# Reordering the recurrent pairs of a two-layer hybrid diffusion trunk: where the next pair's ScalarE work, one corner product and the ada sums are placed

## Chip, cores and metric

The kernel runs on one NeuronCore of one Trainium2 chip, in float32 throughout. The metric is the device time of one execution in microseconds (us), here the median of the runs shown. Engines are named as in the profile: PE (TensorE matmul), PEld (its weight loads), DVE (VectorE), ACT (ScalarE), POOL (GpSimd), SP (SyncE, which issues the weight DMAs). The granted clock of TensorE is at its upper level (2.4 GHz) in nearly the whole run, 0.994 on average.

## What is computed

Two trunk layers over 256 context tokens and 256 latent tokens of width 1024. Each layer modulates and normalises its input, projects it, runs three branches (a short convolution, a two-directional RWKV-7 recurrence, windowed attention), merges them, and ends in a convolved feed-forward. Layer 1 emits the latent tokens only.

```python
mod_l = jnp.split((jax.nn.silu(c) @ p['ada_w'] + p['ada_b'])[:, None, :], 6, axis=-1)
mod_c = jnp.split(jax.nn.silu(c_ctx) @ p['ada_w'] + p['ada_b'], 6, axis=-1)
hl = modulate(xl, p['norm1_g'], mod_l[0], mod_l[1])
...
def step(S, inp):                       # 16 heads, two directions
    rt, wt, kt, vt, at, bt = inp
    sa = jnp.einsum('dbhvk,dbhk->dbhv', S, at)
    S = S * wt[..., None, :] + sa[..., :, None] * bt[..., None, :] + vt[..., :, None] * kt[..., None, :]
...
w_log = -jax.nn.softplus(-w_pre.astype(f)) - 0.5
decay = jnp.exp(-jnp.exp(w_log))
a = jax.nn.sigmoid((p['rwkv_a0'] + jnp.einsum('tdr,drc->tdc', al, p['rwkv_a2'])).astype(f))
...
xl = xl + mod_l[2] * merge_branches(conv_l, rwkv_l, att_l, gate_l, p)
xl = xl + mod_l[5] * conv_ffn(modulate(xl, p['norm2_g'], mod_l[3], mod_l[4]), p)
```

## The kernel before, in words

Activations lie transposed, 128 channels on the partitions and 512 tokens (T) on the free axis, of which layer 1 mostly uses the last 256 (`lo`). Weights come from HBM as strips of 1024x128 through a ring of five buffers; eight matmuls of one strip (`strip_steps`, L453) make one 128-channel output. **The order of every engine's work is written out by hand**, in one block per engine, and the engines meet by semaphores. PSUM is handed out in three rotations of two slots each: A (emptied by ACT), G (dense projections) and P, called Q in the code (pair work, emptied mostly by DVE). `take(F, name)` waits until the slot's last content has been emptied.

*The recurrence* (`mix`) goes over eight pairs of heads. The tokens are cut into eight chunks of 64. For a pair `i` TensorE does, in this order: products of the chunks (`pair_products`, L676), transposes (`turn_hats` L653, `turn_values` L666), `half_step` (slot `w`, L694: 64 products of 32x32 blocks), `corners` (slot `tl`, L704: 64 products; then slot `tr`, L709: 32 products, the second corner product), `below_left` (slot `x10`, L721), `value_products` (slots `mv0`, `mv1`, L744), `corner_below` (slot `t10`, L730), `bonus_sums` (L750), and for the next pair `key_sums` (L621) and `decays` (L628 twice, then `g`, L631), then `through_inverse` (slots `lrb0` to `lrb3`, L762). After that it walks the chunks: `state_out` (L793) and `state_in` (L779) in turn, seven and seven. Between all these stand the next pair's dense strips, cut into pieces: `fill(steps, n)` issues n units, a unit being one matmul of 256 columns, and `hop` is the number of units between two state steps.

ACT empties the A slots (`corners` L1465 for tl, L1467 and L1468 for tr; `value_products` L1478; `corner_below` L1472, L1473; `through_inverse` L1488), centres the next pair's r, k, v (L1402), takes `conv_gate` (L1496) from a G slot, and makes the next pair's decay: `key_norm` (L1409 logarithm, L1411 exponential), a table load (L1306), `decays` (four tanh, L1419, then the copy of `g`, L1425), and, after `through_inverse`, `powers` (L1433, L1434, L1436 for each direction). DVE turns the decay into running sums (`decays`, L1886 and two scans L1889) and then works through `hats`, 19 steps, four steps for each chunk of the walk, between its own state operations (L2077, L2084, L2086, L2088). Layer 0's attention and feed-forward work on ada_w besides: each group of 512 columns is multiplied strip by strip into four 32-row quadrants (`ada_strip`, L514), copied to SBUF by ACT, and `ada_pick` (L533) adds the quadrants with a matmul against a 128x2 table, whose two-column results ACT copies into `mod` (L1338).

The code of the loop's core on TensorE:

```python
half_step(i)
pair_products(1, 0, i)
fill(steps, 10 if wide or not ahead else 4)
corners(i)
pair_products(1, 1, i)
fill(steps, 6 if wide or not ahead else 4)
below_left(i)
value_products(i)
```

## Time and profile before

| what | before |
|---|---|
| median of 3 runs (lowest, highest) | 2956.99 us (2953.68, 2960.45) |
| the profiled execution, its own time | 2950.64 us |
| its span, first to last instruction | 2948.9 us |
| PE busy | 2860.9 us, 97% of the span |
| PEld, DVE, ACT busy | 58%, 43%, 25% |
| DMA traffic | 264.24 MB, mean 90 GB/s |
| PE in the chain that ended last | 90% |

Each float32 product of the program shows as two matmul records and two weight-load records, a transpose as one of each. Stretches of the span: layer 0's pairs about 108 to 785 us, its attention 785 to 1155, the last branch and the output projection to 1320, feed-forward up 1320 to 1662 and down to 1822; layer 1's pairs 1878 to 2425, its attention to 2622, then the same stages at half width. A wait row says which line waited, for whom, and for how long in all; in a timeline row the bracket gives the idle time before it and who ended it, "issue" standing for no releaser that the profile shows.

### The profile page before, as it was taken

What the parts mean: (1) busy time and instruction counts of PE and PEld (TensorE: products, weight loads), DVE (VectorE), ACT (ScalarE), POOL (GpSimd) and SP (SyncE); (2) the same over time, 40 slices, a digit from 0 to 9 for tenths busy, and PEclk for the clock granted to TensorE, in tenths of its full rate; (3) what the DMA queues carried; (4) which work ended last, traced back from release to release, by engine and by line L of the source; (5) the groups of instructions that cost most, each with busy time, mean ns of one, the idle gap of its engine ahead of it and who ended that gap; (6) DMA issues with size and microseconds to landing.
All of it is one profiled execution on the core that took longest, in us unless ns stands there. A gap on an engine that the chain in (4) does not pass through costs nothing.

```text
span 2948.9 us, 57155 instructions
## 1 busy us (share of the span) xinstructions
PE 2860.9 (97%) x25177; PEld 1721.3 (58%) x25177; DVE 1260.5 (43%) x2571; ACT 724.0 (25%) x1453; POOL 48.3 (2%) x76
## 2 busy tenths in 40 slices
PE   7999999999999999999999999999999999999999
PEld 3555555555654554444444444666666677788887
DVE  2566656555322221133333211566666643323551
ACT  3233333322222221011111001344333322211110
POOL 1000000000000000010000000000000000000000
PEclk9999999999999999999999999999999999999999
DMA  7111111111243333244444324212111124344554
GB/s 253 51 43 40 40 47 40 34 43 44 76 114 100 99 102 99 75 114 120 137 130 136 87 79 122 76 48 57 50 53 47 52 49 135 105 129 135 151 151 120
DMA packets 499989, 264.24 MB, mean 90 GB/s; under 512 B 42864, under 2 KB 493888, under 8 KB 499232
## 3 DMA queue, kind: packets, MB, share of 16 engines
q1 hardware_dynamic: 498016, 251.57, 29.9%
q0 software_dynamic: 1728, 9.03, 0.9%
q8 instruction: 200, 3.28, 0.5%
q14 instruction: 45, 0.37, 0.0%
HBM read 255.31 MB, written 5.24 MB: 88 GB/s over the span
## 4 chain that ended last, share of the span: by engine, by line
PE 90%; ACT 4%; DVE 4%; issue 1%; POOL 0%; DMA 0%; POOLq 0%; DVEq 0%; ACTq 0%
PE psum L453 56%; PE psum L1068 8%; PE psum L474 2%; PE psum L676 2%; PE psum L514 1%; PE psum L899 1%; PE psum L887 1%; ACT arena L1488 1%; PE psum L877 1%; PE psum L744 1%; PE psum L779 1%; PE psum L793 1%; PE psum L829 1%; PE psum L762 1%; PE psum L666 1%
## 5 line engine op out<-in xcount | busy, mean ns | idle before, releaser
L453 PE MATMUL psum<-hT,strips 128*128 128x512 f32 (+1 forms) x3968 | 1449.5, 512 | 4.0 <-ACT arena L1496 2.1
L453 PEld LDWEIGHTS psum<-hT,strips 128*128 128x128 f32 x3968 | 726.1, 190 | 504.2 <-issue 433.9
L1068 PE MATMUL psum<-arena,strips 128*128 128x512 f32 (+1 forms) x704 | 227.6, 486 | 0.6 <-DVE arena L2313 0.6
L1068 PEld LDWEIGHTS psum<-arena,strips 128*128 128x128 f32 x704 | 133.7, 190 | 93.5 <-issue 83.5
L453 PE MATMUL psum<-arena,strips 128*128 128x512 f32 (+1 forms) x512 | 167.9, 486 | 2.0 <-DVE done L2193 2.0
L1812 DVE TENSOR_SCALAR arena<-arena 128x512 f32<-128x512 f32 (+1 forms) x88 | 37.0, 420 | 278.9 <-ACT arena L1669 278.8
L1669 ACT COPY arena<-psum 128x512 f32<-128x512 f32 (+1 forms) x88 | 42.2, 480 | 412.2 <-PE psum L453 397.4
L453 PEld LDWEIGHTS psum<-arena,strips 128*128 128x128 f32 x512 | 97.1, 190 | 69.9 <-issue 60.7
L2159 DVE SCALAR_TENSOR_TENSOR arena<-arena,psum 128x512 f32<-128x512 f32 (+1 forms) x32 | 17.7, 554 | 268.1 <-PE psum L453 268.1
L2313 DVE SCALAR_TENSOR_TENSOR arena<-psum,mod,arena 128x256 f32<-128x256 f32 x24 | 10.9, 481 | 194.3 <-PE psum L1068 194.3
L1971 DVE TENSOR_TENSOR arena<-psum,tables 128x1024 f32<-128x1024 f32 x48 | 58.5, 1218 | 77.6 <-PE psum L676 77.6
L453 PE MATMUL psum<-conv_branch,strips 128*128 128x512 f32 (+1 forms) x256 | 85.8, 488 | 1.7 <-ACT arena L1559 1.5
L453 PE MATMUL psum<-rwkv_branch,strips 128*128 128x512 f32 (+1 forms) x256 | 85.2, 486 | 0.0
L474 PE MATMUL psum<-hT,strips 128*128 128x512 f32 (+1 forms) x160 | 72.3, 616 | 11.3 <-ACT hT L1328 11.3
L1532 ACT ACTIVATE arena<-psum,arena 128x512 f32<-128x512 f32 (+1 forms) x96 | 58.2, 613 | 88.5 <-DVE arena L2134 88.0
L779 PEld LDWEIGHTS psum<-arena 64*64 64x64 f32 x896 | 34.8, 133 | 76.6 <-DVE arena L2088 38.9
L676 PE MATMUL psum<-arena 64*128 64x128 f32 (+1 forms) x1024 | 75.9, 287 | 3.5 <-issue 3.5
L1559 ACT ACTIVATE arena<-psum 128x512 f32<-128x512 f32 (+1 forms) x48 | 23.6, 491 | 217.0 <-PE psum L453 217.0
L2077 DVE TENSOR_TENSOR arena<-psum,arena 64x256 f32<-64x256 f32 x112 | 47.2, 421 | 67.8 <-PE psum L779 67.3
L793 PEld LDWEIGHTS psum<-arena 128*64 128x64 f32 x896 | 35.1, 136 | 66.2 <-issue 41.9
L1488 ACT COPY arena<-psum 64x512 f32<-64x512 f32 (+1 forms) x128 | 67.6, 528 | 10.8 <-PE psum L762 9.2
L1872 DVE SCALAR_TENSOR_TENSOR arena<-psum,params,arena 128x510 f32<-128x510 f32 (+1 forms) x48 | 33.7, 701 | 83.5 <-ACT arena L1402 83.0
(247 smaller groups left out, 3216.0 us busy)
## 6 DMA issues: line engine op xcount, KB each, us to landing
strips<-in_w_in_dram SPq DMA_DIRECT2D x158, 512.0 KB, 4.0
strips<-in_ffn_up_dram SPq DMA_DIRECT2D x88, 512.0 KB, 4.3
strips<-in_ada_w_dram SPq DMA_DIRECT2D x80, 512.0 KB, 4.1
strips<-in_ffn_down_dram SPq DMA_DIRECT2D x32, 512.0 KB, 4.0
arena<-in_ada_w_dram SPq DMA_DIRECT2D x4, 2048.0 KB, 14.6
strips<-in_w_in_dram SPq DMA_DIRECT2D x32, 256.0 KB, 3.8
strips<-in_a_out_w_dram SPq DMA_DIRECT2D x16, 512.0 KB, 4.1
strips<-in_rwkv_out_w_dram SPq DMA_DIRECT2D x16, 512.0 KB, 4.1
```

The source lines that it names most:

```text
L453: ins = mm(s.o[:, first:T], strip[:, b, k, :], rhs[:, k, first:T], k == 0, k == KT - 1)
L474: ins = mm(ss[j].o[:, first:T], strip[:, bs[j], k, :], hT[:, k, first:T], k == 0, k == KT - 1)
L676: ins = one(PS[:, b0 + h, (c % 4) * n:(c % 4 + 1) * n], BK[d][rows(h), c].rearrange("p j t -> p (j t)"), ar[d][rows(h), c, 0:n // CH].rear ...
L779: ins = one(PS[r, BANK_P[s.b] + h, d * CH:(d + 1) * CH], AR[i % 2][d][rows(h), c, 0, :], GG[rows(h), c, d, :])
L793: ins = one(PS[rows(h), BANK_P[s.b], d * CH:(d + 1) * CH], EE[:, 2, c // 4, d, h, c % 4, :], RV[:, c, d, h, :])
L1068: ins = mm(s.o[:, lo:T], strip[:, b, j, :], hid[:, k, lo:T], k == 0, k == FT - 1)
L1488: ins = act.copy(EE[r, k0:3, m // 2, :, :, 2 * (m % 2) + p].rearrange("p k d h t -> p k (d h) t").rearrange("p k q t -> p q k t"), PS[r, B ...
L1532: ins = act.activation(pr[u][:, x:x + 2 * T // g], PS[:, b0 + x // T, x % T:x % T + 2 * T // g], ACT.Exp, bias=st[:, u, 1, i:i + 1], accum ...
L1669: act.copy(upp[:, b, lo // SEG:, 1:SEG + 1], s.o[:, lo:T].rearrange("p (s t) -> p s t", t=SEG)).then_inc(s.free, 1)
L1812: ts(dst, src[:, :, 1:n + 1], g1, None, MUL).then_inc(s_vec, 1)
L1971: tt(EE[:, 0:2, j, d].rearrange("p k h c t -> p k (h c) t").rearrange("p k q t -> p q k t"), o, mask.unsqueeze(1).broadcast_to([P, 8, 2, C ...
L2077: tt(dst, o, add, ADD).then_inc(s.free, 1)
```

## The change

Four edits, all in the hand-written orders; what is computed stays the same.

1. *The next pair's decay earlier.* `decays` is split. Its two products (`decay(0)`, `decay(1)`) stand after `pair_products(1, 1)` and after the fill behind it; ACT takes their four tanh between tl's and tr's copies; `powers(0)` and `powers(1)` stand around `corner_below`'s copies, ahead of `conv_gate` and `key_norm`; DVE's scans (now `sums`) lie on either side of `below_left`. ACT's two table loads per pair move: one to before tl's copy, one to before `powers(0)`. `g` (now `gate_in`) stays where it was. DVE does four steps of `hats` before the walk.
2. *The second corner product* (`corners_right`) stands behind `below_left`, directly ahead of `value_products`.
3. `bonus_sums` moves up behind `pair_products(1, 0)`; in layer 1 the last fill before `through_inverse` is 2 units instead of 4, and `hop` is 2.15 instead of 2.
4. *The ada sums in batches.* Four groups' quadrant sums are kept in SBUF and added at once: `pick_rows` (four matmuls of 512 columns, each into one 32-row quadrant) and, after a copy by ACT, `pick_turn` (four transposes). Five batches take the place of 16 half picks and 12 group picks.

```diff
-    cols["pick"] = p[:, None] % 32 == np.arange(2)[None, :]
+    cols["pick"] = (p[:, None] % 32 == np.arange(32)[None, :]) & (np.arange(32)[None, :] < 2)
...
-            def pick_half(l, g, e):
-                ada_pick(A, (l, g, e), part_blocks(part_att, 2 * e, 2 * e + 2))
+            def pick_rows(F, l, b, ready, sums):
+
+                pe.wait_ge(*ready.freed)
+                s = take(F, "rows", l, b)
+                for q in range(4):
+                    ins = one(s.o[quad(q)], tab["pick"], sums[:, q, :])
+                ins.then_inc(s.full[0], 1)
+
+            def pick_turn(F, l, b):
+
+                pe.wait_ge(*slots["rows", l, b].freed)
+                s = take(F, "turned", l, b)
+                for m in range(4):
+                    ins = pe.transpose(s.o[:, m * P:(m + 1) * P], picked[:, m * P:(m + 1) * P], tab["ident"])
+                ins.then_inc(s.full[0], 1)
...
-                if m % 4 == 1 and g > 0:
-                    ada_pick(G, (1, g - 1), part_blocks(part[:, 0, :], 0, 4))
+                if m % 16 == 1 and g > 0:
+                    pick_rows(G, 1, g // 4 - 1, slots["ada", 1, g - 1], sums_ffn)
+                if m % 16 == 3 and g > 0:
+                    pick_turn(G, 1, g // 4 - 1)
...
                     pair_products(1, 0, i)
+                    bonus_sums(i)
                     fill(steps, 10 if wide or not ahead else 4)
                     corners(i)
                     pair_products(1, 1, i)
+                    if ahead:
+                        decay(0, i + 1)
                     fill(steps, 6 if wide or not ahead else 4)
+                    if ahead:
+                        decay(1, i + 1)
                     below_left(i)
+                    corners_right(i)
                     value_products(i)
                     fill(steps, 4 if wide or not ahead else 3)
                     corner_below(i)
-                    bonus_sums(i)
                     fill(steps, 4 if wide or not ahead else 5)
                     if ahead:
                         key_sums(i + 1)
-                        decays(i + 1)
-                        fill(steps, 4)
+                        gate_in(i + 1)
+                        fill(steps, 4 if wide else 2)
                     through_inverse(i, ahead)
-                    hop = (3.7 if ahead else 4) if wide else 2 if ahead else 2.3
+                    hop = (3.7 if ahead else 4) if wide else 2.15 if ahead else 2.3
...
                     if i > 0:
                         head_inverse(i - 1)
+                        if ahead:
+                            exps_and_tanhs()
                     corners(i)
+                    if ahead:
+                        decay(0, i + 1)
+                        decay(1, i + 1)
+                    corners_right(i)
                     value_products(i)
                     if ahead:
                         centre(1, "k", i + 1, 0)
+                        logs()
+                        powers(0, i + 1)
                     else:
                         keys(1)
                     corner_below(i)
                     if ahead:
+                        powers(1, i + 1)
                         if lo:
                             conv_gate(i + 1)
                         key_norm(i + 1)
-                        decays(i + 1)
+                        gate_in(i + 1)
                     through_inverse(i)
                     if ahead:
                         if lo == 0:
                             conv_gate(i + 1)
-                        powers(0, i + 1)
-                        powers(1, i + 1)
                         conv_centre(i + 1)
...
+            EARLY_HATS = 4
...
                     if i > 0:
                         normed(i - 1)
+                    bonus(i)
                     masked_pairs(1, 1, i)
+                    if ahead:
+                        decays(i + 1)
+                        sums(0)
                     below_left(i)
                     if ahead:
+                        sums(1)
                         s = taps(1, "k", i + 1, 0, 1)
                         key_squares(i + 1, s)
-                    bonus(i)
                     state_in(0, i)
-                    if ahead:
-                        decays(i + 1)
                     steps = hats(i + 1) if ahead else iter(())
+                    for _ in range(EARLY_HATS):
+                        next(steps, None)
```

The order on PE in a pair of layer 1, from the end of the first `pair_products` of direction 1 to `through_inverse`. Before (L704 is tl, L709 tr, L721 x10, L744 mv0 and mv1, L730 t10, L750 the bonus, L621 the key sums, L628 the two decay products, L631 g):

```order
L704 MATMUL psum<-arena 32x32 x64
L709 MATMUL psum<-arena 32x32 x32
L676 MATMUL psum<-arena 128x128 x8
L453 MATMUL psum<-hT,strips 128x512 x2
L721 MATMUL psum<-arena 32x32 x32
L744 MATMUL psum<-arena 64x64 x32
L453 MATMUL psum<-hT,strips 128x256 x3
L730 MATMUL psum<-arena 32x32 x32
...
L628 MATMUL psum<-low_rank,low_rank_out 128x512 x4
L631 MATMUL psum<-low_rank,low_rank_out 128x256
L453 MATMUL psum<-hT,strips 128x256 x4
L762 MATMUL psum<-arena 64x64 x16
```

With the change (L725 is tl, L647 a decay product, L745 x10, L733 tr, L768 mv0 and mv1, L754 t10, L640 the key sums, L652 g, L786 `through_inverse`):

```order
L725 MATMUL psum<-arena 32x32 x64
L697 MATMUL psum<-arena 128x128 x8
L647 MATMUL psum<-low_rank,low_rank_out 128x512 x2
L457 MATMUL psum<-hT,strips 128x512 x2
L647 MATMUL psum<-low_rank,low_rank_out 128x512 x2
L745 MATMUL psum<-arena 32x32 x32
L733 MATMUL psum<-arena 32x32 x32
L768 MATMUL psum<-arena 64x64 x32
...
L640 MATMUL psum<-arena,tables 128x512
L652 MATMUL psum<-low_rank,low_rank_out 128x256
L457 MATMUL psum<-hT,strips 128x256 x2
L786 MATMUL psum<-arena 64x64 x16
```

tr has left tl's side and stands between x10 and mv; the decay products have left the place between the key sums and g.

ACT at the same place. Before, from mv1's side on (L1402 centres k, L1472 empties t10, L1496 is `conv_gate`):

```order
L1478 COPY arena<-psum 128x512 x2
L1402 ACTIVATE arena<-psum,params 128x512
L1472 COPY arena<-psum 32x16x32
L1473 COPY arena<-psum 32x16x32
L1496 COPY arena<-psum 128x256
L1409 ACTIVATE arena<-psum,tables 128x512
L1411 ACTIVATE arena<-arena 128x512
L1306 ACT_TABLE_LOAD
L1419 ACTIVATE arena<-psum,params 128x512
...
L1425 COPY arena<-psum 128x256
L1488 COPY arena<-psum 64x4x64 x4
```

With the change (L1521 is mv0 and mv1, L1443 centres k, L1476 to L1479 are `powers`, L1515 empties t10, L1539 is `conv_gate`, L1450 and L1452 the key norm, L1468 the copy of g):

```order
L1521 COPY arena<-psum 128x512 x2
L1443 ACTIVATE arena<-psum,params 128x512
L1338 ACT_TABLE_LOAD
L1476 ACTIVATE arena<-arena 128x8x64
...
L1515 COPY arena<-psum 32x16x32
L1516 COPY arena<-psum 32x16x32
L1476 ACTIVATE arena<-arena 128x8x64
...
L1539 COPY arena<-psum 128x256
L1450 ACTIVATE arena<-psum,tables 128x512
L1452 ACTIVATE arena<-arena 128x512
L1468 COPY arena<-psum 128x256
L1531 COPY arena<-psum 64x4x64 x4
```

The four tanh have gone from between the key norm and the copy of g; a table load and both `powers` now stand ahead of `conv_gate`, the key norm and that copy.

## Rows read from the trace of the kernel before

**Rows 1.** The page: busy time, and the queue of kind instruction (packets, MB, share)

```profile
PE 2860.9 (97%) x25177; PEld 1721.3 (58%) x25177; DVE 1260.5 (43%) x2571; ACT 724.0 (25%) x1453; POOL 48.3 (2%) x76
...
q8 instruction: 200, 3.28, 0.5%
```

**Rows 2.** Stretches: length, busy of PE, PEld, DVE, ACT, POOL, clock, DMA share, GB/s

```profile
785.00:1155.00 370.00, 369.13 (x1721) 182.56 (x1720) 100.93 (x251) 94.17 (x274) 0.00 (x0) 1.00 0.38 107
...
1320.00:1662.00 342.00, 341.20 (x1385) 153.75 (x1386) 124.90 (x223) 50.92 (x100) 1.84 (x4) 1.00 0.45 129
1880.00:2425.00 545.00, 516.68 (x8705) 359.30 (x8704) 345.47 (x694) 196.20 (x358) 14.72 (x18) 0.99 0.18 50
```

**Rows 3.** Waits of PE in the whole run: total us, times, longest us

```profile
PE psum L709 <- issue: 11.0, 8, 2.1
...
PE psum L779 <- DVE arena L2088: 5.2, 21, 0.4
PE psum L762 <- ACT arena L1425: 4.7, 7, 1.4
...
PE psum L676 <- issue: 3.5, 3, 1.5
```

**Rows 4.** Timeline of PE: the picks, and products of the new forms

```profile
19.78 1.92 PE L506 MATMUL psum<-arena,tables 128*32 128x512 f32 x16
...
876.07 1.09 PE L887 MATMUL psum<-tables,arena 128*128 128x128 f32 x8
...
883.87 0.50 PE L533 MATMUL psum<-tables,arena 128*128 128x2 f32 x4
884.30 1.13 PE L877 MATMUL psum<-arena 64*128 64x512 f32 x4
...
1398.08 1.05 PE L533 MATMUL psum<-tables,arena 128*128 128x2 f32 x8
1399.00 1.53 PE L453 MATMUL psum<-hT,strips 128*128 128x512 f32 x3
```

**Rows 5.** Timeline of PE: two pairs around the second corner product

```profile
302.81 1.18 PE L709 MATMUL psum<-arena 32*32 32x32 f32 x63
...
2104.99 1.27 PE L704 MATMUL psum<-arena 32*32 32x32 f32 x127
...
2108.12 1.08 PE L709 MATMUL psum<-arena 32*32 32x32 f32 x54 [1.69 <-issue]
...
2114.82 2.08 PE L744 MATMUL psum<-arena 64*64 64x64 f32 x64
```

**Rows 6.** Timeline of PE in the same pair, decay products to `through_inverse`

```profile
2123.10 1.99 PE L628 MATMUL psum<-low_rank,low_rank_out 64*128 64x512 f32 x8
...
2125.55 1.89 PE L453 MATMUL psum<-hT,strips 128*128 128x256 f32 x8
2127.37 0.68 PE L762 MATMUL psum<-arena 64*64 64x64 f32 x16
2128.61 2.62 PE L762 MATMUL psum<-arena 64*64 64x64 f32 x48 [0.55 <-ACT arena L1425]
```

**Rows 7.** Timeline of ACT in the same pair, and one row of DVE

```profile
2109.23 0.58 ACT L1467 COPY arena<-psum 32x512 f32<-32x512 f32 x1 [2.33 <-PE psum L709]
...
2119.57 0.58 ACT L1472 COPY arena<-psum 32x512 f32<-32x512 f32 x1 [1.45 <-PE psum L730]
...
2122.35 0.37 ACT L1496 COPY arena<-psum 128x256 f32<-128x256 f32 x1 [1.61 <-PE psum L453]
2123.21 0.69 ACT L1409 ACTIVATE arena<-psum,tables 128x512 f32<-128x512 f32 x1 [0.49 <-PE psum L621]
...
2124.57 1.28 ACT L1306 ACT_TABLE_LOAD   x1
2125.87 2.42 ACT L1419 ACTIVATE arena<-psum,params 128x512 f32<-128x512 f32 x4
...
2134.19 0.69 DVE L1921 SCALAR_TENSOR_TENSOR arena<-arena 128x512 f32<-128x512 f32 x1 [0.60 <-ACT arena L1436]
```

More of the change, by code:

```diff
@@ L532, in ada_pick @@
                 for m, v in enumerate(blocks):
-                    ins = one(s.o[:, 2 * m:2 * m + 2], v, tab["pick"])
+                    ins = one(s.o[:, 2 * m:2 * m + 2], v, tab["pick"][:, 0:2])
                 ins.then_inc(s.full[0], 1)
@@ L621, in key_sums, with decay, gate_in @@
                     one(s.o, tab["heads"], rinv_k).then_inc(s.full[0], 1)
-                def decays(i):
-                    pe.wait_ge(*lr.full())
-                    for q in range(2):
-                        s = take(Q, f"decay{q}", l, i)
-                        for h in range(2):
-                            ins = one(PS[:, BANK_P[s.b] + h, :], lw[rows(h), q, :], low[rows(h), q, :])
-                        ins.then_inc(s.full[0], 1)
+                def decay(q, i):
+                    if q == 0:
+                        pe.wait_ge(*lr.full())
+                    s = take(Q, f"decay{q}", l, i)
+                    for h in range(2):
+                        ins = one(PS[:, BANK_P[s.b] + h, :], lw[rows(h), q, :], low[rows(h), q, :])
+                    ins.then_inc(s.full[0], 1)
+                def gate_in(i):
                     s = take(A, "g", l, i)
@@ L922, in attend @@
                                 pass
-                        if t > 0 and ATT_ADA[l]:
-                            pick_half(l, ATT_ADA[l][t - 1], 1)
+                        if t == 4 and ATT_ADA[l]:
+                            pick_rows(A, l, 1, slots["ada", l, ATT_ADA[l][3], 1], sums_att)
                         scores(t, 0)
@@ L935, in attend @@
                         branch(0, t)
+                        if t == 4 and ATT_ADA[l]:
+                            pick_turn(A, l, 1)
                         if ATT_ADA[l]:
@@ L951, in attend @@
                     if ATT_ADA[l]:
-                        pick_half(l, ATT_ADA[l][KT - 1], 1)
+                        pick_rows(A, l, 2, slots["ada", l, ATT_ADA[l][KT - 1], 1], sums_att)
                     gate(2, 0)
                     weighted(KT - 1, 1)
+                    if ATT_ADA[l]:
+                        pick_turn(A, l, 2)
                     for n in range(KT):
@@ L989, in mix @@
                 pe.wait_ge(s_late, 16)
+                if l == 1:
+                    pick_turn(A, 1, 2)
                 key_sums(0)
                 pe.wait_ge(ev["low_ready"], l + 1)
-                decays(0)
+                decay(0, 0)
+                decay(1, 0)
+                gate_in(0)
                 pe.drain().then_inc(lr.free, 1)
@@ L1096, in _ @@
                 if l == 1:
-                    ada_pick(G, (1, 11), part_blocks(part[:, 0, :], 0, 4))
+                    pick_rows(A, 1, 2, slots["ada", 1, 11], sums_ffn)
                 mix(l, lo)
@@ L1571, in attend @@
                             query(t + 2)
[L1572 to L1573 removed]
+                        if t == 4 and ATT_ADA[l]:
+                            picked_rows(l, 1)
                         if t > 0:
```

107 lines of the change are left out of this document (60 added, 47 removed).

## The prediction

> **What bounds the kernel now.** The page comes first: TensorE (PE) is busy for 97% of the span [rows 1]. A busy PE says little about what can still be won, so the table of stretches is read next. In layer 0's attention PE stands idle for 0.9 us of 370, in its feed-forward for 0.8 of 342, but in layer 1's pairs for 28.3 of 545, while DVE and ACT are busy for 63% and 36% of that stretch and the DMA engines for 18% [rows 2]. So in the first two stretches only work taken off PE counts, and in the pairs the waits count as well. Which waits these are is in PE's list: 11.0 us at the second corner product (L709) and 3.5 us at the line behind it (L676), in 8 and 3 pairs of 16, both with no releaser; 5.2 us of `state_in` for DVE (L2088); 4.7 us of `through_inverse` for ACT's copy of `g` (L1425) [rows 3]. The timelines then tell what each of them is made of, and there the reader should look at the number in brackets.
>
> Each cost below is a change of PE's time, since no other engine is near the bound.
>
> **The ada sums.** A half pick keeps PE from 883.87 to 884.30, 0.43 us; a group's pick from 1398.08 to 1399.00, 0.92 us [rows 4]. The change removes 16 of the first (6.9 us) and 12 of the second. One of the twelve, group 0's, stands ahead of the feed-forward's first products, where PE waits for the normalised input anyway; that leaves 11 (10.1 us). In their place come five batches. `pick_rows` is four products, eight records, of the form of L506 (128 rows, 32 columns of weights, 512 columns moved, in four quadrants), of which 16 take 1.92 us, so 0.96; `pick_turn` is four transposes, half of the eight that take 1.09 at L887, so 0.55 [rows 4]. Five times 1.5 is 7.5 us. The sum is 17.0 - 7.5, **9.5 us less**. The copies on ACT become fewer and lie under the dense strips, where ACT has room (94 us busy of 370 [rows 2]): nothing. If the other quadrants' work were not done side by side as in L506, `pick_rows` would cost eight times the 0.43 us of a 512-column record and the gain would be gone; the row of the same form decides, and I keep 7 to 10 as the bounds.
>
> **The idle time without a releaser.** In the row of the second corner product 54 of its 64 records start after 1.69 us in which PE had nothing to do, 3.13 us after the first corner product began (2104.99 to 2108.12) [rows 5]. In another pair the same 64 records run through in 1.18 us [rows 5], so it is not a semaphore that is always late. The page has a queue of kind instruction with 200 packets and 3.28 MB [rows 1]: 16.4 KB each, and with 2 x 25177 records of PE, one packet for about 250 of them. tl's 64 products are 256 records (a product has two matmuls and two weight loads) and pass in 1.2 us, so PE uses up a packet's worth in that time, and the next is there about 3.1 us after the last was begun. I read the idle time as waiting for instructions. Between `half_step` and the end of tr there are about 680 records in some 6 us of PE's own time. The change takes tr's 128 away from there and puts them after x10, ahead of mv. The run x10, tr, mv is three times 128 records in about 4.2 us (1.1, 1.1 and 2.0 [rows 5]): 2.2 to 2.8 us a packet instead of 1.2. What is short of 3.1 us is then 0.3 to 0.9 where it was 1.9, about a third, and behind tl there now follow 2 us of `pair_products`, 1 us of decay product and 1.9 us of fill, which is room. Two thirds of the 14.5 us is 9.7. Since the packets' borders shift with every edit and will catch more of the other small products than now, I take **7 us less**, with 0 and 14.5 as the ends.
> The Trainium skill, "Runtime: NRT & Kernel Launch", section on instruction fetch mechanics, says that instructions come in blocks of 16 KiB (256 instructions) and that crossing a block's border is mostly hidden. The block size agrees with the 16.4 KB above; the second half does not agree with 11.0 us at L709. By the page this term would be zero.
>
> **The second corner product's slot.** mv1 takes the A slot that tr held. Before, tr's two copies (0.58 us each, start 0.11 after tr's last record [rows 5, 7]) had 6 us; now mv1 is wanted 1.0 us after tr's end, and the slot is free after 0.11 + 1.17 + 0.04, 1.3 us. That is 0.3 us in each of 16 pairs, 5 us; where waiting for instructions falls into mv it costs nothing on top, in about six pairs. I take **3 us more** (0 to 5). The four tanh ahead of these copies are no danger: they are done 1.2 us after the second decay product, and x10 and tr take 2.2.
>
> **ACT's chain to `g`, layer 1.** Before, `through_inverse` waits 0.55 us for the copy of `g`, which stands behind the key norm, a table load (1.28 us) and four tanh (2.42) [rows 6, 7]. These 3.7 us leave the place. But PE is there earlier too: two decay products (1.9 us of the 2.45 up to the fill) and two units of fill (0.9) are gone as well [rows 6]. And ACT gets a table load and both `powers` (1.3 us each) ahead of the key norm, 3.9 us, where it idled 1.45 + 1.61 + 0.49, 3.55 us, before [rows 7]; with `bonus_sums` (0.6 us) moved up, PE comes to the key sums earlier by that. From the end of mv1 I get 8.5 us for ACT up to the end of `g`'s copy and 7.7 us for PE up to the second product group of `through_inverse`. The wait is then 0.8 instead of 0.55, shared between `conv_gate`'s G slot and `g`'s: **2 us more** over seven pairs (0 to 7). In layer 0 the fills are longer (1.8 us for the last, and `g` is wanted a microsecond later than ACT has it), so nothing.
>
> **The walk, layer 1.** DVE starts `hats` when the walk starts, has to wait 0.60 us for `powers` [rows 7], and its steps keep the state operations waiting: 21 waits of up to 0.4 us, 5.2 us in all [rows 3]. With `powers` and scans done before and four of 19 steps ahead, DVE has 2.5 us less to do in the walk and no wait in it. I take **4 us less** (0 to 5.2). In layer 0 a step of the walk is 1.7 us of fill and hides this already.
>
> `bonus_sums` costs the same at its new place, and the units taken from the last fill are issued in the walk: zero.
>
> **Sum.** -9.5 - 7 + 3 + 2 - 4 is -15.5 us. The profiled execution took 2950.64 us, so 2935.1; the median of the three runs lies 6.35 us above that execution, so 2941.5, and I forecast **2942 us**.
>
> **Rivals.**
> 1. *The waits for instructions only move.* A run of 384 records is still longer than a packet, and if every pair is caught at the new place, term two is zero: 2949 us. For it: 11 of 16 pairs are caught now. Against: the new run is slower per record. (The page's rule gives the same number for another reason, that there was nothing to gain; the row speaks against that reason.) 0.17.
> 2. *The walk and the instruction waits both clear fully*: -9.5 - 12 + 2 - 5, 2932 us. 0.12.
> 3. *Only the picks count.* ACT's later copies eat what the pairs win; the reordering comes to zero: 2947.5 us, 0.13.
> 4. *ACT becomes the bound of the pairs, slower.* In each pair ACT now has 3.9 us more between mv1 and the key norm; if this comes late by 1.2 us (a tanh waiting for the decay product, a table load that can't start under a copy), conv_gate, the key norm and `rinv` are late, DVE's early steps start late, and `through_inverse` waits 1.5 to 2 us in 14 pairs: +24, +5 for tr's slot, no gain in the walk, -9.5: +19, 2976 us. It decides once the extra wait passes 1.1 us a pair. Against: ACT is busy for only 36% [rows 2]. 0.06.
>
> **Chances.** The forecast's own case has 0.52, its range from the terms' ends is 2936 to 2949. A measurement of this kernel can tell about 0.2%, 6 us, from no change, so faster means below 2951. The forecast's case, case 2, most of case 3 and three quarters of case 1 lie there: 0.79. Within 0.2%: 0.14. Slower: case 4 and a little beside, 0.07. The range of 8 in 10 is 2932 to 2954.
>
> **What would show it.** In the changed kernel's list of PE's waits: L733 and the line behind it with little "issue" time, `value_products` (L768) with a few waits of 0.5 to 1 us of it, and 0.3 us for ACT's L1511 in the other pairs; `state_in` (L803) with under 2 us; in layer 1 about 0.8 us a pair for L1539 and L1468; picks' lines with under 8 us on PE. The forecast is wrong if the stretch of layer 0's attention and feed-forward up doesn't get shorter by some 7 us, or if the pairs of either layer get longer.

## The result, and the profile after

| | before | after |
|---|---|---|
| median (lowest, highest) | 2955.34 us (2950.90, 2960.45), 4 runs | 2924.58 us (2920.91, 2926.39), 4 runs |
| ratio | | 0.9896, 95% interval 0.9878 to 0.9914 |
| profiled execution, its span | 2950.64, 2948.9 us | 2925.36, 2923.6 us |

The change makes the kernel 30.8 us faster, twice the 15.5 us of the forecast's sum, and the time lies outside the range. The sign and the places were right, the size was not.

The page after, the lines of [rows 1]:

```profile
PE 2845.0 (97%) x25077; PEld 1704.4 (58%) x25077; DVE 1269.2 (43%) x2571; ACT 722.8 (25%) x1431; POOL 52.0 (2%) x76
...
q8 instruction: 200, 3.28, 0.5%
```

PE's waits after, those that answer to [rows 3] (L733 is the second corner product, L803 `state_in`, L786 `through_inverse`, L768 mv0 and mv1, L835 and L842 `outputs`, L457 a dense strip):

```profile
PE psum L457 <- ACT arena L1539: 7.2, 14, 0.7
PE psum L786 <- ACT arena L1531: 6.2, 16, 0.4
PE psum L768 <- ACT arena L1511: 2.8, 15, 0.2
PE psum L842 <- issue: 2.3, 4, 1.0
PE psum L835 <- issue: 1.9, 2, 1.0
PE psum L768 <- issue: 0.7, 2, 0.5
...
PE psum L733 <- issue: 0.4, 1, 0.4
```

The second corner product has lost its 11.0 us, and `state_in` has no row left. What is new: 5.1 of the 7.2 us at L1539 (the slot that ACT's `conv_gate` empties), 3.7 more at L1531 (the copies of `through_inverse`), and the 2.8 at L1511 that the prediction priced at 3. Before, the first two were these:

```profile
PE psum L762 <- ACT arena L1488: 2.5, 9, 0.4
PE psum L453 <- ACT arena L1496: 2.1, 7, 0.3
```

The picks, as in [rows 4], in the feed-forward after (L548 `pick_rows`, L556 `pick_turn`):

```profile
1417.97 1.04 PE L548 MATMUL psum<-arena,tables 128*32 128x512 f32 x8
...
1435.09 0.63 PE L556 MATMUL psum<-tables,arena 128*128 128x128 f32 x4 [0.80 <-ACT arena L1369]
```

1.0 and 0.6 us, as costed, and twice in the run a wait of 0.8 us for ACT's copy between them. From the start of layer 0's last pair to the start of layer 1's first, PE goes from 1179.7 to 1171.9 us (in the second profiled execution of each, further down, from 1180.7 to 1169.0).

The stretches of the pairs, from the first `diagonal_blocks` of a layer to its eighth (in [rows 2] layer 1's stood with other bounds). Before, layer 0 and layer 1:

```profile
107.43:697.98 590.55, 572.47 (x7999) 321.62 (x7999) 349.46 (x626) 194.71 (x325) 11.36 (x13) 0.99 0.15 41
1877.66:2356.61 478.95, 451.75 (x7663) 309.15 (x7662) 317.44 (x632) 178.28 (x325) 11.99 (x14) 0.99 0.18 51
```

After:

```profile
109.35:691.50 582.15, 567.03 (x7999) 319.74 (x7998) 353.10 (x626) 195.84 (x324) 13.03 (x13) 1.00 0.15 42
1863.36:2330.92 467.56, 448.80 (x7663) 307.44 (x7663) 321.94 (x632) 178.85 (x324) 13.58 (x14) 0.99 0.19 52
```

PE issues the same instructions in the same number in both. Seven pairs of layer 0 take 8.4 us less, of which only 3.0 are idle time (18.1 to 15.1); the other 5.4 are PE's *busy* time, with no work taken away. That is the first sign of something that the prediction's list of waits doesn't hold: matmuls that ran longer before. (3.4 of the 5.4 are the half clock of the next section; most of the rest is that the decay products take 0.2 us a pair less at their new place, see the last part.) Layer 1's pairs take 11.4 us less, 8.4 of it idle time.

### The profile page after: what moved, and what is told of

Read it like the earlier page. It is cut to its first block, busy times and chain, and to the rows that moved or that the text cites. A ratio compares the mean times of both kernels' runs of the same rounds, so it can differ in the third digit from the quotient of the medians.

```text
span 2923.6 us, 56943 instructions
## 1 busy us (share of the span) xinstructions
PE 2845.0 (97%) x25077; PEld 1704.4 (58%) x25077; DVE 1269.2 (43%) x2571; ACT 722.8 (25%) x1431; POOL 52.0 (2%) x76
## 4 chain that ended last, share of the span: by engine, by line
PE 92%; ACT 4%; DVE 2%; issue 1%; DMA 0%; SPq 0%; DVEq 0%; ACTq 0%
PE psum L457 57%; PE psum L1103 8%; PE psum L478 3%; PE psum L697 2%; PE psum L817 1%; PE psum L803 1%; PE psum L518 1%; PE psum L923 1%; PE psum L786 1%; PE psum L911 1%; PE psum L901 1%; PE psum L853 1%; PE psum L647 1%; PE psum L687 1%; PE psum L842 1%
## 5 line engine op out<-in xcount | busy, mean ns | idle before, releaser
L457 PE MATMUL psum<-hT,strips 128*128 128x512 f32 (+1 forms) x3968 | 1446.3, 511 | 9.1 <-ACT arena L1539 7.2
L457 PEld LDWEIGHTS psum<-hT,strips 128*128 128x128 f32 x3968 | 724.1, 190 | 521.5 <-issue 445.9
L457 PE MATMUL psum<-arena,strips 128*128 128x512 f32 (+1 forms) x512 | 167.9, 486 | 2.0 <-DVE done L2251 2.0
L457 PEld LDWEIGHTS psum<-arena,strips 128*128 128x128 f32 x512 | 97.1, 190 | 69.9 <-issue 60.7
L2217 DVE SCALAR_TENSOR_TENSOR arena<-arena,psum 128x512 f32<-128x512 f32 (+1 forms) x32 | 17.8, 555 | 264.8 <-PE psum L457 264.8
L457 PE MATMUL psum<-conv_branch,strips 128*128 128x512 f32 (+1 forms) x256 | 85.8, 488 | 1.7 <-ACT arena L1602 1.5
L457 PE MATMUL psum<-rwkv_branch,strips 128*128 128x512 f32 (+1 forms) x256 | 85.2, 486 | 0.0
L803 PEld LDWEIGHTS psum<-arena 64*64 64x64 f32 x896 | 34.8, 133 | 70.0 <-issue 36.8
L1531 ACT COPY arena<-psum 64x512 f32<-64x512 f32 (+1 forms) x128 | 67.6, 528 | 18.1 <-PE psum L786 16.3
```

What stands on the lines that cost most here:

```text
L457: ins = mm(s.o[:, first:T], strip[:, b, k, :], rhs[:, k, first:T], k == 0, k == KT - 1)
L803: ins = one(PS[r, BANK_P[s.b] + h, d * CH:(d + 1) * CH], AR[i % 2][d][rows(h), c, 0, :], GG[rows(h), c, d, :])
L1531: ins = act.copy(EE[r, k0:3, m // 2, :, :, 2 * (m % 2) + p].rearrange("p k d h t -> p k (d h) t").rearrange("p k q t -> p q k t"), PS[r, B ...
```

## What bounds the places: the theory before the experiments

Two things can be read beside the rows. First, where in PE's own list of records (two matmuls and two weight loads a product, one of each for a transpose, and the semaphore records ahead of a wait) the idle times without releaser stand. Counted in program order, all of before's but one (0.26 us at the start of layer 1) lie at 192 modulo 256. The reading is that 256 records at a time come in, and PE stands where the next block has not come. With one block per 3.5 us at the soonest, begun some 48 records before it is needed, the count says for every order of the program which product will be caught, and by how much. I fitted these two numbers to the first trace, so they say nothing about it; the experiments test them.

Second, the granted clock. In the pair of [rows 5] the granted clock falls to 0.50 (of its two levels, 2.4 and 1.2 GHz, the lower) just behind the idle time. Another such place of before, after 1.71 us of idle time at 557.80:

```profile
557.50:559.40 1.90, 1.60 (x38) 1.43 (x37) 0.00 (x0) 1.03 (x2) 0.00 (x0) 1.00 0.04 9
559.40:562.80 3.40, 3.40 (x5) 1.40 (x5) 1.23 (x1) 0.12 (x1) 0.00 (x0) 0.50 0.00 0
562.80:566.20 3.40, 3.40 (x109) 2.55 (x109) 1.14 (x2) 0.08 (x1) 0.00 (x0) 1.00 0.02 5
```

The seventh column is the clock. By an estimate, 3.40 us at half clock is 1.7 us of PE's work that is not done. None of this stands among PE's waits, since PE is busy in it.

**Theory A**: beyond the picks, the gain is mostly that the second corner product no longer lengthens the run of small products behind the first, by fewer waits for instructions and less time at half clock. **Rival B**: the gain is the next pair's decay leaving ACT's and DVE's late part of the pair.

## The experiments

Each set of kernels ran beside the kernel before on one chip; the kernel before took 2953.9 to 2955.4 us in all of them. "Idle" is PE's idle time without a releaser (gaps over 0.15 us, between 110 and 2450 us of the span), "half clock" the time at clock 0.50 in the two layers' pairs, both from the profiled execution. The last row rests on two executions.

| kernel | median us | ratio, 95% interval | idle | half clock |
|---|---|---|---|---|
| before (first execution) | 2955.34 | | 17.8 | 13.6 |
| before, second execution | 2954.65 | 0.9995 (0.9986 to 1.0004) | 18.3 | 30.6 |
| picks alone | 2949.69 | 0.9976 (0.9965 to 0.9987) | 19.4 | 23.8 |
| picks and second corner's place | 2937.23 | 0.9932 (0.9919 to 0.9945) | 7.3 | 13.6 |
| picks and decay early | 2939.89 | 0.9944 (0.9931 to 0.9957) | 19.6 | 27.2 |
| the change (first execution) | 2924.58 | 0.9896 (0.9878 to 0.9914) | 6.1 | 6.8 |
| the change, second execution | 2922.36 | 0.9888 (0.9869 to 0.9908) | 8.7 | 10.2 |
| before + 48 products | 2970.41 | 1.0054 (1.0039 to 1.0070) | 26.5 | 34.0 |
| before + 1024 products | 3015.78 | 1.0204 (1.0181 to 1.0227) | 45.7 | |

### One part of the change at a time

*Picks alone.* Edit 4 on the kernel before.

> The kernel before with edit 4 alone (ada sums in batches), the pairs as they were. All theories: the picks' own gain, 8.4 us by the two traces' stretches (9.5 in the prediction). Theory A (idle time without a releaser is waiting for the next block of 256 records): the edit takes 218 records away from PE between the layers, so layer 0 keeps its idle times (second corner product of pairs 0 and 5) and layer 1's move to other pairs: 1.8 us ahead of or in the second corner product of pairs 0, 1, 4 and 5, and none in pairs 3 (they were in 0, 3, 4 and smaller ones in 1, 2, 5); in all 17.7 us instead of 16.2, so about 7 us faster than before (2948). Rival B (these idle times belong to what a pair computes or to its data): they stay in the pairs where they were, 8.4 us faster (2947).

Measured: 5.7 us by the medians, 3.8 to 10.3 by the interval; the stretch from layer 0's last pair to layer 1's start is 8.2 us shorter. The idle time is 19.4 us, and layer 1's stands now in pairs 0, 1, 4 and 5 (2.11, 1.97, 2.22 and 1.74 us), the four that theory A named, and no longer in 3. Not a line of the pairs was touched; 218 records fewer ahead of them moved it. The last of the four:

```profile
2244.80 0.53 PE L733 MATMUL psum<-arena 32*32 32x32 f32 x11 [1.74 <-issue]
```

*Picks and the second corner product's place* (edits 1 and 3 undone; the lines are against the change):

```diff
                     corners_right(i)
                     value_products(i)
                     fill(steps, 4 if wide or not ahead else 3)
                     corner_below(i)
+                    bonus_sums(i)
...
                         key_sums(i + 1)
+                        decay(0, i + 1)
+                        decay(1, i + 1)
                         gate_in(i + 1)
-                        fill(steps, 4 if wide else 2)
+                        fill(steps, 4)
```

> The changed kernel with edits 1 and 3 undone (decay, scans, powers, bonus, fills and hats as before), so edit 4 and the second corner product's new place alone. Theory A (most of the gain beyond the picks comes from this move: less waiting for records, and no half-clock stretches behind it): picks -8.4, idle time without releaser from 17.5 to at most 9, half-clock stretches in the pairs gone (-5), the second value product's wait for its slot +2.8: about 19 us faster than before (2936), and idle times of 0.5 to 1 us in value_products of layer 1's pairs 0, 1, 4 and 5 instead of 1.8. Rival B (the gain comes from the decay's move): 8.4 - 2.8, 5.6 us faster (2950). state_in's waits for DVE stay at 5 us and through_inverse's for g near 4.7 in both.

Measured: 18.1 us faster than before, against theory A's 19. But the half-clock time of this profiled execution, 13.6 us, is the same as in the first of before, where A had it gone; 10.2 of it stand at the start of layer 1, behind PE's first wait there for DVE. The idle times of 0.5 to 1 us in `value_products` came in two of the four named pairs (1.41 and 0.60 us). The idle time is 7.3 us, and in the waits `state_in` and the copy of `g` are as before:

```profile
PE psum L803 <- DVE arena L2140: 5.2, 21, 0.4
PE psum L786 <- ACT arena L1465: 4.7, 7, 1.4
...
PE psum L768 <- ACT arena L1510: 3.6, 13, 1.4
...
PE psum L768 <- issue: 2.2, 3, 1.4
```

*Picks and the decay early* (edit 2 undone):

```diff
                     corners(i)
+                    corners_right(i)
                     pair_products(1, 1, i)
...
                     below_left(i)
-                    corners_right(i)
                     value_products(i)
```

> The changed kernel with the second corner product back behind the first (edit 2 undone), edits 1, 3 and 4 kept. Theory A: idle time without releaser back to 17 us, ahead of the second corner product in pairs 0 and 5 of layer 0 and 0, 1, 4 and 5 of layer 1, 1.8 us each, with half-clock stretches behind some of them; the mv1 wait gone (-2.8); 14 to 17 us slower than the changed kernel, about 11 to 14 us faster than before (2943). Rival B: 2.8 us faster than the changed kernel, 28 us faster than before.

Measured: 15.5 us faster than before, 15.3 slower than the change with the second corner product in its new place. Idle is back at 19.6 us, half clock at 27.2. B alone falls; but A does not have it alone either. With the picks in, the corner's place is worth 12.5 us (2949.7 to 2937.2) and the decay 9.8 (2949.7 to 2939.9), each with some 5 us of uncertainty, and together 25.1 (2949.7 to 2924.6).

One profiled execution says little about the half clock, but every execution's mean granted clock is on record, and with it its time at half clock in the whole span: on average 50 us with the picks alone (9 executions) and 49 with the decay early (6), against 34 with the corner at its new place and the old decay (5). It is the corner's place that takes half clock away.

### Is the idle time a wait for blocks of records?

*48 products more*, at one place in the whole kernel before, in pair 0 of layer 0:

```diff
+                    if (l, i) == (0, 0):
+                        for t in range(12):
+                            for q in range(4):
+                                one(PS[quad(q), b0, t * 32:(t + 1) * 32], LC[quad(q), t, :], T16[quad(q), t, :])
```

> The kernel before with 48 of the 64 products of half_step issued twice in pair 0 of layer 0 only: 192 records and 0.9 us of PE more, nothing else. Theory A: every later record's place in its block of 256 moves by 192, so the idle times without releaser move: out of pairs 0 and 5 of layer 0 (134 and 558 us) and 0, 3, 4 of layer 1, into half_step of pair 0 (2.2 us), the second corner product of pairs 1, 2, 6, 7 of layer 0 and 2, 3, 6, 7 of layer 1 (1.3 to 1.8 each) and pair_products of pairs 0 and 5 of layer 0 and 0 and 4 of layer 1 (about 1); in all 24.8 us instead of 16.2, so with the 0.9 about 9.5 us slower than before, more if half-clock stretches follow. Rival B (the idle times belong to the pair): same pairs, 0.9 us slower.

Measured: 15.0 us slower for 0.9 us of work. The idle times moved as counted, from end to end of the kernel: half_step of pair 0 1.97 us, the second corner product of pairs 1, 2, 6, 7 (1.77, 2.02, 1.70, 1.94) and, 1700 us later, of pairs 2, 3, 6, 7 of layer 1 (2.11, 1.87, 1.47, 1.91), `pair_products` in the four named pairs with 0.92 to 1.07. One of 1.27 in pair 3 of layer 0 was not forecast. A row of a pair that had none before:

```profile
313.17 0.85 PE L713 MATMUL psum<-arena 32*32 32x32 f32 x42 [2.02 <-issue]
```

Idle rises by 8.7 us, half clock by 20.4 over the first execution of before (10.2 us of work) and 3.4 over the second. So the place in the block decides which pair pays.

The same count, made in the traces of every kernel of this document, finds each idle time without releaser between 110 and 2450 us at 192 modulo 256, but for the 0.26 or 0.27 us at the start of layer 1. The transfers of the queue of kind instruction are in the traces too: packets of 16384 bytes, 0.9 to 1.8 us each. In before, picks alone, + 48 products, + 1024 products and the change, every such idle time over 0.3 us ended 1.2 to 1.6 us after one of these packets had ended.

*1024 products more*, the same loop 16 times over all 64:

> The kernel before with half_step's 64 products issued 16 times more in pair 0 of layer 0: 1024 products of 32x32, 4096 records, 16 blocks of 256, nothing else; the places of all later records in their blocks stay. Theory A (a block of records takes about 3.4 us to come, whatever it holds): 16 x 3.4 = 54 us, plus at most 3, so about 3010 us, and the row of these products shows an idle time of 2 to 2.4 us at each 64th product, all other idle times without releaser where they were. Rival (PE goes through them at the pace at which half_step's 64 pass, 1.2 us): 16 x 1.2 = 19 us, 2975.

Measured: 60.9 us slower. A timeline of PE in the added products, and the queue's line of the page:

```profile
130.72 1.27 PE L695 MATMUL psum<-arena 32*32 32x32 f32 x128 [2.26 <-issue]
134.17 1.93 PE L695 MATMUL psum<-arena 32*32 32x32 f32 x128 [2.18 <-issue]
137.63 1.93 PE L695 MATMUL psum<-arena 32*32 32x32 f32 x128 [1.52 <-issue]
...
q8 instruction: 216, 3.54, 0.5%
```

Sixteen packets more for 4096 records, 16 x 256. From the second row on the clock is at 0.50 (for 58 us), and each 64 products take 1.93 instead of 1.27 us, and by the third the idle time has shrunk by as much: a row still begins 3.45 us after the one before. The pace is that of the blocks and not of PE. Five steps are 3.73 us and one is 4.00; in four of the five the instruction packet took 1.23 to 1.34 us, where it took 0.9 to 1.1 in those of 3.45. The other idle times stand in the pairs where they were. The rival's 19 us is out.

### What the time at half clock does

The kernel before, unchanged, once more.

> The kernel before, unchanged, for a second profiled execution and more runs: its profiled execution (2950.64 us) lies 4.7 us under the median of all its runs. If that distance is time at half clock behind the idle times, which not every execution shows at the same pairs, this execution, at about 2955, has more than the 39.6 us at half clock of the first (some 48), and the same idle times without releaser (17.5 us, same pairs). If it is noise of the start (DMA), the stretches of the pairs are the same to 1 us and the start is longer. The ratio should be 1.000.

Measured: the second profiled execution of before took 2961.82 us, 11.2 more than the first, with the same idle (18.3 against 17.8 us, the large ones in the same pairs) and at half clock 55.9 us in the whole span instead of 37.7 (the 39.6 of the expectation runs past the last instruction), 30.6 instead of 13.6 in the pairs. The stretch behind the second corner product of layer 1's pair 4 shows it; first execution, then second:

```profile
2178.41 0.56 PE L709 MATMUL psum<-arena 32*32 32x32 f32 x23 [1.98 <-issue]
...
2179.99 1.98 PE L453 MATMUL psum<-hT,strips 128*128 128x512 f32 x4
```

```profile
2188.13 0.85 PE L709 MATMUL psum<-arena 32*32 32x32 f32 x23 [2.16 <-issue]
...
2190.92 3.59 PE L453 MATMUL psum<-hT,strips 128*128 128x512 f32 x4
...
2187.40:2194.20 6.80, 6.07 (x43) 3.67 (x43) 1.22 (x1) 1.16 (x2) 0.00 (x0) 0.50 0.01 2
```

The same four records take 1.98 us once and 3.59 the other time. From `half_step` to `value_products` this pair takes 12.70 us in the first execution and 15.69 in the second, and a pair without idle time there takes 10.53. So an idle time of 2 us costs 2.2 us once and 5.2 the other time.

The first half of the expectation holds: of the 11.2 us, 7.4 are in layer 1's pairs, which have 17.1 us more at half clock. Of the second only that the start is longer, by 3.8 us; it has 6.8 us more at half clock itself. Layer 0's pairs are the same to 0.1 us. Over 60 executions of before on record, time and half clock (from each one's mean granted clock) go together, 0.47 us for each us at half clock; with half of it taken off, the times' standard deviation falls from 3.7 to 1.5 us. On average they have 45.8 us of it, the eight of the change 30.7, so half clock makes some 7.5 us of the gain by half of the difference. The times of before here scatter over 14 us (2947.9 to 2961.8, 12 executions), those of the change over 6 (2920.4 to 2926.4, 8 executions).

Not all half clock stands behind an idle time without releaser. PE waits 2.6 to 2.8 us for DVE ahead of the first `half_step` of layer 1, and 3.4 to 6.8 us at half clock followed in all four profiled executions of before and the change.

### What the change still leaves

*Early steps of `hats` left out* (`EARLY_HATS = 0`).

> The changed kernel with no step of hats ahead of the walk instead of four (decay, sums and powers early as they are). If the walk's gain in layer 1 needs these four steps (2.5 us of DVE a pair), state_in waits for DVE again, some 2 to 5 us in all, and the kernel takes 2926 to 2930. If having sums and powers done before the walk was enough, no such waits and no change, 2924.6.

```diff
-            EARLY_HATS = 4
+            EARLY_HATS = 0
```

Measured: 2922.52 us against 2922.36 for the change in the same set. Seven waits of `state_in` came back, 1.3 us; that is below what the runs can tell. By the rows, having sums and powers done before the walk was the larger part (5.2 to 1.3 us).

```profile
PE psum L803 <- DVE arena L2146: 1.3, 7, 0.2
```

The change itself, run beside it:

> The changed kernel as it is, for more runs beside the two below: 2924.6 us again, all theories.

*The second corner product ahead of `below_left`:*

```diff
-                    below_left(i)
-                    corners_right(i)
+                    corners_right(i)
+                    below_left(i)
                     value_products(i)
```

> The changed kernel with the second corner product ahead of below_left instead of behind it (both still behind the second decay product). Its slot is then emptied while below_left runs, so mv1's wait for ACT's copies (2.8 us in 15 waits) goes; idle time without a releaser stays at 5 to 10 us, since the run of 384 records is the same. If the wait for the slot is what the move cost: 2.8 us less, 2922. If blocks of records limit that run anyway: no change, 2925.

Measured: 2920.59 us (ratio to before 0.9882, 0.9865 to 0.9899). The L1511 row is gone, but L768's idle without releaser went from 0.7 to 3.4 us: where PE no longer waits for ACT, it gets to the next block sooner. With L733 counted in, 1 to 2.3 us came back in this way (3.4 against 1.1 and 2.4 in the change's two executions), and the clean pairs of layer 0 (those without idle time of this kind) take 82.84 us instead of 83.21. So part of the slot's cost had been cover for a block, but not all of it; 2 to 4 us faster by the medians is near the 2.8 expected and within the scatter.

*`powers(1)` of layer 1 on ACT behind `through_inverse`:*

```diff
                     if ahead:
-                        powers(1, i + 1)
                         if lo:
                             conv_gate(i + 1)
+                        else:
+                            powers(1, i + 1)
                         key_norm(i + 1)
...
                         if lo == 0:
                             conv_gate(i + 1)
+                        else:
+                            powers(1, i + 1)
```

> The changed kernel with powers(1) of layer 1 on ACT behind through_inverse, as before, instead of ahead of conv_gate. Theory (layer 1's new waits for conv_gate, 5.1 us, and for lrb's copies are ACT's chain made longer by powers(1), 1.4 us): the wait for L1539's copy in layer 1 goes (-5), g's copy is wanted at about its end, and the walk keeps its gain because DVE wants powers(1) some 4 us later than ACT has it: 4 to 5 us less, 2920. Rival (the walk's gain came from powers(1) being early): state_in waits for DVE again, up to 5 us, sum zero, 2925.

Measured: 2918.08 us (0.9873, 0.9858 to 0.9889), where 2920 was expected. The wait for L1539 falls back to layer 0's, no `state_in` row comes, and the copies' wait at L1531 stays:

```profile
PE psum L786 <- ACT arena L1531: 6.1, 16, 0.4
...
PE psum L457 <- ACT arena L1539: 2.1, 7, 0.3
```

ACT's timeline in a pair of the change says why: both `powers` stand ahead of the copy that PE waits for, and its product has been ready all along (no bracket).

```profile
2105.50 0.63 ACT L1476 ACTIVATE arena<-arena 128x512 f32<-128x512 f32 x1
2106.04 0.20 ACT L1477 ACTIVATE arena<-arena 128x8 f32<-128x8 f32 x1
2106.27 0.63 ACT L1479 ACTIVATE arena<-arena 128x512 f32<-128x512 f32 x1
2106.93 0.37 ACT L1539 COPY arena<-psum 128x256 f32<-128x256 f32 x1
```

*Both:*

> Both of the last two edits: 2.8 and 4.5 us less than the changed kernel, 2917. If either only moves a wait to the next instruction, the sum of what the two show alone.

Measured: 2913.20 us (0.9857, 0.9843 to 0.9870), idle 9.2 us; 4 us less than expected, so neither edit merely moved a wait.

*Both, and the run broken*, PE's order being second corner product, second decay product, `below_left`, `value_products`:

```diff
+                    corners_right(i)
                     if ahead:
                         decay(1, i + 1)
                     below_left(i)
-                    corners_right(i)
                     value_products(i)
```

> powers_late with the second corner product ahead of the second decay product, so that the run of 384 records (second corner product, below_left, value_products) is broken by 1 us of large products, on ACT with its copies between the two pairs of tanh. If the pace of blocks is what holds that run, the idle time without releaser in value_products goes and only that in the walk and outputs of some pairs stays, 4 to 6 us in all instead of 9 in both_late; the mv1 wait is gone as well: 2 to 4 us less than both_late, about 2910. If the blocks are no limit there: the same as both_late, 2913.

Measured: 2908.67 us (0.9845, 0.9828 to 0.9862), idle 5.1 us. No row of L768 is left. In pair 3 of layer 1 the change had this row (L733 then stood behind `below_left`):

```profile
2097.10 0.84 PE L733 MATMUL psum<-arena 32*32 32x32 f32 x41 [0.40 <-issue]
```

and here `below_left` (L745) and both value products go through without a bracket:

```profile
2087.43 1.13 PE L647 MATMUL psum<-low_rank,low_rank_out 64*128 64x512 f32 x4
2088.49 1.20 PE L745 MATMUL psum<-arena 32*32 32x32 f32 x64
2089.62 2.08 PE L768 MATMUL psum<-arena 64*64 64x64 f32 x64
```

It beats both kernels: 1.5% under the one before, and about 14 us under the change in the same set of runs.

## Why the prediction was wrong

By its own steps, from the two profiled executions of each kernel (the means, 2956.2 and 2925.4, differ by the medians' 30.8 us). Fixed points of the program are used where they can be: a clean pair takes the same time to some 0.02 us in every execution.

| step | forecast us | measured us |
|---|---|---|
| ada sums | -9.5 | -9.7 (1180.2 to 1170.5 between the layers' pairs) |
| idle time without a releaser | -7 | -10.7 (18.0 to 7.4) |
| half clock | not in the sum | -6.8, an estimate (half of 22.1 less half of 8.5) |
| second corner product's slot | +3 | +4.3 (0.31 in each of 14 pairs; the rows list 2.8 in all) |
| decay products at their new place | 0 | -2.7 (0.19 in each of 14 pairs) |
| ACT's chain in front of and in `through_inverse`, layer 1 | +2 | +3.6 |
| the walk, layer 1 | -4 | -8.9 |
| what lies before and behind | 0 | +0.7 |
| sum | -15.5 | about -30 |

**Ada sums: right.** On average the gain is that of the sum within 0.2 us (7.8 between the first executions, 11.6 between the second). The two forms cost 1.0 and 0.6 us; the 0.8 us wait for the copy between them (twice) was missed.

**Idle time without a releaser: the mechanism right, the term too small.** I took "two thirds" of 14.5 us and gave 2.7 back for borders that would catch other small products. Which products can be caught depends on the order alone, and could have been counted from the program, at 192 modulo 256. That count is worth more than a share by feel. The pace was a little off as well: I read 3.1 us a block from one row, and it is 3.45.

**The step that failed is the one that is not there: half clock.** The 3.4 us at clock 0.50 stood in the trace of before, in the very pair of [rows 5], and I priced an idle time at its own length. Of the 15 us that the sum lacks it makes 6.8; the walk makes 4.9, the idle times themselves 3.7. Two rows of PE in the trace of before would have shown it, `pair_products` behind the second corner product in that pair and in the next:

```profile
2109.12 2.08 PE L676 MATMUL psum<-arena 64*128 64x128 f32 x16
...
2178.90 1.16 PE L676 MATMUL psum<-arena 64*128 64x128 f32 x16
```

The same 16 records, 0.92 us apart, and no wait between. How often it happens differs between executions of one kernel (13.6 and 30.6 us before), so that one profile could not have given the mean either. Of the 22.1 and 8.5 us in the table, 17.1 and 1.7 follow an idle time without releaser, the rest the wait for DVE at the start of layer 1. The range was narrower than the terms under it besides: their own lower ends (-10, -14.5, 0, 0, -5.2) add up to 2927, not to the 2936 that is called their end.

**The slot: the price right, the number of pairs too low.** A clean pair of layer 0 is 0.3 us longer with the corner at its new place (83.10 to 83.39 us with the old decay, 82.90 to 83.21 with the early one), which was the price, but in all pairs and not in ten. That it hardly shows in layer 0 (83.11 before, 83.21 after) is luck: the decay's two products cost 2.11 us at their old place and 1.92 at the new one (what the stretches ahead of `value_products` and of `through_inverse` gain and lose, with `bonus_sums` taken off at 0.86), a term that the sum put at zero.

**ACT's chain: right in kind, the term too small.** The prediction looked at the copy of `g` and shared a wait of 0.8 us a pair between that and `conv_gate`. It is 0.7 us a pair at `conv_gate` alone, while the wait for `g` is gone and one of 0.4 us for the first `lrb` copies has come. By fixed points, the stretch from `corner_below` to `through_inverse` holds 0.99 us of waiting a pair (6.63 us, against 5.64 with `powers(1)` late), and the one from there to the walk is 0.36 us shorter than before, 1.19 in pair 0: 3.6 in seven. (The wait rows give 3.9 over both layers: 4.7 us gone, 4.9 and 3.7 come.)

**The walk: a good part of its gain was not in the list of waits.** In the kernel with the old decay the waits of `state_in` in pair 2 of layer 1 are 0.36, 0.20 and 0.18 us, and there are gaps between that are too short for a row. From the walk's first `state_out` to the next pair PE takes 20.99 us instead of 21.39, and has two units of fill more in it (0.43 us each): 1.27 us less per pair, 8.9 in seven, against 5.2 in the row. Where many short gaps are in question the distance of two fixed points of the program is the measure, not the sum of listed waits.

**The rivals.** Case 2 (both clear fully, 2932) was nearest and still 7 us off. Case 1 (the waits only move) fell: they moved, and shrank. Case 3 (only the picks count) fell: the picks alone stand at 2949.7, 25 us above the change. Case 4 (ACT becomes the bound) has its mechanism in the L1539 row, at a quarter of its deciding price (3.6 us over 14 pairs, 0.26 a pair against 1.1). The page's rule that crossing a block's border is mostly hidden (the Trainium skill, "Runtime: NRT & Kernel Launch", instruction fetch mechanics) would have put both the second and the missing step at zero; the block size of 256 that the same section gives is what the experiments show. In stretches of large products the sentence holds: from 785 to 1155 us PE is idle for 0.9 us in all [rows 2].

That the corner's place and the decay are worth 3 us more together than one by one is within the scatter, and open. No run here shows why an idle time is followed by half clock in one execution and not in the next.

## What to carry to other kernels

A run of many small products is limited by the pace at which instructions arrive: here 3.45 us per 256 records (64 float32 products), against 1.27 us of PE's work for them. Break such runs with a few large products, place the breaks by counting records, and expect that any edit ahead moves the cost to other places. An idle time of two microseconds may cost 3 us more in half clock, seen only in busy times. A gap filled by one wait may in part be another wait's cover, so test fixes in pairs. Where the order is written by hand, the distance of two fixed points in a pair without disturbance prices an edit to some 0.02 us, where the intervals of the medians here are 3 to 6 us to either side.

## What the runs showed of the hardware

- One block of instructions is 256 records (16 packets more for 4096), and the next one came 3.45 us after the last at the soonest, sometimes 3.73, once 4.00, at either level of the clock. PE went on 1.2 to 1.6 us after the packet's end.
- An edit of 192 records in one place moved the later idle times of the whole kernel to other pairs and cost 15 us for 0.9 us of work.
- Behind idle times of 1 to 2.8 us the granted clock was 0.50 for 3.4 or 6.8 us in some executions and not in others, at the same place: 13.6 and 30.6 us in the pairs of one and the same kernel. It explains most of the scatter of the kernel before (45.8 us on average in 60 executions, 0.47 us of time for each).
